# A gate block ahead of the latent attention's first scores, and one fewer behind its last

## The reference, cut to what matters

```python
z = h @ w_in + b_in            # 34 column chunks of 128, then four gates of 1024 columns
y_a = gmlp(u, v)               # spatial mixing within chunks of 128 tokens
y_b = short_conv(cb, cc, ch)
y_c = mla(q_lat, kv_lat, k_rope)   # latent attention: 8 heads, causal, query/key width 96, value width 64
y_d = nsa(nq, ...)                 # sparse attention: 16 head units
merged = sigmoid(ga)*y_a + sigmoid(gb)*y_b + sigmoid(gc)*y_c + sigmoid(gd)*y_d
mix = merged @ w_o
```

## Time and profile before

| | us |
|---|---|
| median of 3 runs | 2861.49 |
| lowest and highest | 2860.31, 2862.87 |
| the profiled execution's own time | 2865.89 |
| its span, first to last instruction | 2864.0 |
| TensorE busy in the span | 2712.1 (95%) |
| GpSimd busy | 2202.7 (77%) |
| ScalarE busy | 1492.4 (52%) |
| VectorE busy | 1359.3 (47%) |
| mean granted TensorE clock | 0.975 of full speed |

### The profile page before, as it was taken

The page is one execution under the profiler, slowest core; times in us unless marked ns, Lnnn a source line. Parts: engine busy times, 40 slices in busy tenths (PEclk is TensorE's granted clock), DMA queues, the critical chain, the costliest instruction groups (busy, mean ns, idle before and its releaser), DMA issues.

```text
span 2864.0 us, 60059 instructions
## 1 busy us (share of the span) xinstructions
PE 2712.1 (95%) x21781; PEld 2618.4 (91%) x21788; DVE 1359.3 (47%) x2507; ACT 1492.4 (52%) x2261; POOL 2202.7 (77%) x1681
## 2 busy tenths in 40 slices
PE   8999999999999999999999989998999899898997
PEld 8999988889999989998889989998999899788997
DVE  2125435646556554435556554246533533735334
ACT  4444445555555545455455554457544644555445
POOL 7875766757988967666758978978899699667994
PEclk9999999999999999999999999999999999999998
DMA  6554434434554544434434544544555455444552
GB/s 239 185 169 145 147 119 138 149 125 148 187 179 155 184 147 166 135 131 134 162 118 155 184 154 155 183 150 159 166 185 182 140 191 183 133 134 149 187 183 80
DMA packets 123000, 452.12 MB, mean 158 GB/s; under 512 B 13650, under 2 KB 13650, under 8 KB 122196
## 3 DMA queue, kind: packets, MB, share of 16 engines
q1 hardware_dynamic: 121104, 441.43, 46.3%
q10 hardware_dynamic: 1732, 8.39, 0.8%
HBM read 448.72 MB, written 1.05 MB: 157 GB/s over the span
## 4 chain that ended last, share of the span: by engine, by line
POOL 60%; issue 31%; PE 7%; POOLq 1%; DVE 0%; ACT 0%; DVEq 0%; ACTq 0%
POOL wl L373 31%; POOL wl L374 29%; PE R L412 2%; PE R L408 2%; PE R L411 2%; PE Y L408 1%; PE Y L412 1%; PE Y L411 1%; POOLq L379 0%; PE R L571 0%; POOLq L377 0%; DVE BL L1917 0%; DVE X L2042 0%; PE R L435 0%; ACT wh L1142 0%
## 5 line engine op out<-in xcount | busy, mean ns | idle before, releaser
L373 POOL TENSOR_TENSOR wl<-raw,wh 128x512 fp32r<-128x512 f32 x836 | 1111.8, 1330 | 636.8 <-ACT wh L1142 630.4
L408 PE MATMUL R<-XHB,wh 128*128 128x256 f32 (+1 forms) x4168 | 1191.5, 286 | 16.2 <-DVE XLB L2296 6.2
L412 PE MATMUL R<-XHB,wl 128*128 128x256 f32 (+1 forms) x4168 | 1182.3, 284 | 0.0
L411 PE MATMUL R<-XLB,wh 128*128 128x256 f32 (+1 forms) x4168 | 1178.5, 283 | 0.0
L374 POOL TENSOR_TENSOR wl<-raw,wh 128x512 fp32r<-128x512 f32 x836 | 1142.6, 1367 | 0.0
L1142 ACT ACTIVATE wh<-raw 128x1024 fp32r<-128x1024 f32 x836 | 877.1, 1058 | 300.2 <-PE R L408 219.9
L408 PEld LDWEIGHTS R<-XHB,wh 128*128 128x128 f32 x4168 | 792.6, 190 | 23.9 <-POOL wl L374 10.5
L411 PEld LDWEIGHTS R<-XLB,wh 128*128 128x128 f32 x4168 | 795.8, 191 | 1.8 <-issue 1.0
L412 PEld LDWEIGHTS R<-XHB,wl 128*128 128x128 f32 x4168 | 794.2, 191 | 0.0
L408 PE MATMUL Y<-BH,wh 128*128 128x256 f32 x1408 | 398.0, 283 | 1.3 <-DVE BL L1841 1.3
L412 PE MATMUL Y<-BH,wl 128*128 128x256 f32 x1408 | 396.4, 282 | 0.0
(11 more groups left out here) (409 smaller groups left out, 3204.6 us busy)
## 6 DMA issues: line engine op xcount, KB each, us to landing
raw<-in_stream SPq DMA_DIRECT2D x836, 512.0 KB, 3.3
G<-in_wcmp ACTq DMA_DIRECT2D x2, 2048.0 KB, 7.7
G<-in_mem ACTq DMA_DIRECT2D x2, 1024.0 KB, 5.9
TB<-in_table SPq DMA_DIRECT2D x1, 1312.0 KB, 12.8
X<-in_x SPq DMA_DIRECT2D x2, 512.0 KB, 5.9
out_dram<-X ACTq DMA_DIRECT2D x4, 256.0 KB, 2.2
WS<-in_mix_w ACTq DMA_DIRECT2D x2, 256.0 KB
G<-in_p ACTq DMA_DIRECT2D x2, 256.0 KB, 3.3
```

Source lines behind the costliest of these rows:

```text
L373: pool.tensor_tensor(wl[:, s, 0:512], raw[:, r, 0:512], wh[:, s, 0:512].bitcast(F32), ALU.subtract)
L408: i = pe.matmul(o, wh[w], hi, start=start, stop=False, skip_group_check=True)
L411: pe.matmul(o, wh[w], lo, start=False, stop=False, skip_group_check=True)
L412: i = pe.matmul(o, wl[w], hi, start=False, stop=stop, skip_group_check=True)
```

## The change

On TensorE one gate block is issued in front of the waits that precede the first scores, and the last head's filler has one block in place of two. The number of blocks and their order in the stream stay as they are, and so do the lists of all other engines.

```diff
+                dense(XH, XL)
                 pe.wait_ge(q_up, l + 1)
                 pe.wait_ge(kv_up, l + 1)
                 for b in range(4):
                     pe.wait_ge(aside_taken[b], ((l + 1) * len(ASIDE) - b + 3) // 4)
-                attention_pairs([mla_unit(h) for h in range(8)], lambda u: (dense(XH, XL), dense(XH, XL)))
+                attention_pairs([mla_unit(h) for h in range(8)], lambda u: [dense(XH, XL) for _ in range(2 if u < 7 else 1)])
```

## The result

The change took 2872.33 us (median of 7 runs, 2870.62 to 2877.22), the kernel before 2864.38 in the runs it is compared with (2860.31 to 2870.28). The ratio is 1.0033, with a 95% interval of 1.0023 to 1.0043, so +6.6 to +12.3 us. Forecast were +5.8 and 2867.3 in a range up to 2870.5. The time came out 5.0 above the forecast: 2.9 because before, in these runs, has a median of 2864.38 and not the 2861.49 that the forecast started from, and 2.1 because the medians lie 7.95 apart and not 5.8. Its profiled execution took 2872.33, span 2870.4; that of before 2865.89 and 2864.0.

A forecast was written before the change was run, and what follows sets the result against it. TensorE's own work was taken to set the pace inside the attention. Stalls less gains, +4.1 over both layers, plus one clock fall of 1.7 gave +5.8 on a median of 2861.5: 2867.3 us, range 2860.5 to 2870.5.

The forecast's parts named there:

- The gain of the moved block, 4.6 and 4.3: Before the second pair's transposes: us gained in first and second layer if nothing stalls, 8.9 together.
- The added wait at the third block, caused by ScalarE's list: In every pair TensorE waits for GpSimd's half of a block ScalarE rounds only after the exponentials; eight waits, about 2.5 or 1.2.
- The stall of 2.53 in the first pair: First layer, third block: ready at 379.78, wanted at 377.41, plus 0.16 for pick-up and a longer first matmul.
- 1.9 and 1.2 in the later pairs: Third-block stalls: 1.9 us in the first layer's second pair, 1.2 in each other later pair of both layers.
- One clock fall, 1.7, with bounds 0 and 3.4: Behind the first pairs' stalls TensorE's clock falls in one of two layers, adding 1.7 us.
- the rival with a fall in both layers: The stalls plus a clock fall in each layer: +7.5, 2869.0 us; chance 0.22.
- The sum of the stages, +5.8: Both attention stages: stalls less gains, +4.1, and one clock fall, 1.7, make the execution 5.8 us longer.
- The stage has no slack, and what the attention loses is passed on in full: Behind the attention TensorE sets the pace, so the attention's whole loss, +5.8 us, reaches the total.
- the difference is put on the median: 2867.3: The +5.8 was added to the median of the runs shown, 2861.5, not to the profiled execution.
- The bound of 5.7 us for faster, same, slower: What a measurement of the total can tell from no change, about 0.2%; the +5.8 lay on it.

The follow-up runs named there:

- a_5: The change unaltered, its fifth profiled execution: 2867.80 us, stages 67.53 and 68.94.
- first3: The change with the block in front taken from the first pair (three blocks there), not the last: 2864.06 against 2864.04, ratio 1.0005.
- layer0: The kernel before with the change in the first layer alone: 2865.25 against 2864.04, ratio 1.0005.
- layer1: The kernel before with the change in the second layer alone: 2867.40 against 2861.74, ratio 1.0025.
- the filled kernel: The change with ten matmuls of zeros on TensorE in front of the first pair's third block: 2870.13 against 2861.74, ratio 1.0030.
- Pad: The kernel before with twelve matmuls of zeros behind the latent attention in each layer: 2870.18 against 2861.74, ratio 1.0031.
- pad16: The kernel before with sixteen matmuls of zeros behind the first layer's latent attention alone: 2861.81 against 2863.00, ratio 1.0001.
- b_3: The kernel before, unchanged, its third profiled execution: 2861.29 us, stages 64.62 and 66.07.
- b_5: The kernel before, unchanged, its fifth profiled execution: 2855.34 us, stages 64.64 and 65.91.

## Why the prediction was wrong, step by step

- *The gain of the moved block, 4.6 and 4.3.* Right: without stalls the stages are 8.8 shorter, for 8.9.
- *The added wait at the third block, caused by ScalarE's list.* Right in cause and place: eight waits for L374, none when ScalarE's list moves along, one per layer when only the first pair leads.
- *The stall of 2.53 in the first pair.* Right: 2.24 idle and 0.16 for the pick-up and the longer first matmul, 2.40. The next transposes were put 0.80 later than before. Counted from the eviction of chunk 33 they came 0.85 later in a_5, where the clock stayed up, and 2.4 later in the first trace, where it fell.
- *1.9 and 1.2 in the later pairs.* The 1.9 was mis-sized: in before g7's second half ends 9.32 behind its own pair's scores (394.49 - 385.17), in the change 8.60 (394.44 + 1.27 - 387.11), as g11's does in before (408.43 - 399.81 = 8.62). From scores to scores a pair takes 402.84 - 387.11 = 15.73 in the change and 14.64 before, so each costs 1.1.
- *One clock fall, 1.7, with bounds 0 and 3.4.* Mis-sized: there were two, as in the rival with a fall in both layers, which had a chance of 0.22. The clock fell behind 13 of the 14 unfilled first-pair waits in the traces of the change, its four repeats, first3, layer0 and layer1. Each costs 1.5, by the filled kernel.
- *The sum of the stages, +5.8.* It was measured as +5.8 in the first pair of traces and as +6.2 over five of each. That it fits is luck: a second fall that was not in the sum, and later pairs that cost less than the sum had for them, cancelled each other.
- *"The stage has no slack, and what the attention loses is passed on in full", and "the difference is put on the median: 2867.3".* This is the step that failed, in two terms. The first is the clock in all the other stages, which the sum has at nothing, from one trace. It was not the same: the mean granted clock was 0.9780 before and 0.9756 in the change, which goes with 3.6 us; the 5.8 of the stages did arrive, as 6.9 (5.8 to 8.1) at the same clock. Pad shows the same without any stall: 5.0 in the stages, 8.4 in the total. The second is the median of three runs, 2861.49, taken with their 2.6 us as the kernel's spread. The later runs of before go from 2855 to 2870, and the median in the comparison was 2864.38. On that one the same +5.8 gives 2870.2, and the same range would have ended at 2873.4, above the measured 2872.33.
- *The bound of 5.7 us for faster, same, slower.* The forecast lay on it and the chances were split nearly evenly between same and slower; it came out slower.

What stays open is why the mean clock of the change is lower. The largest surplus found in a single stretch, the compression's, is not tied to the change, and a bare delay moved the mean clock both down (pad) and up (pad16).

## What to carry to other kernels

When one engine's work is moved forward by a unit, look at the lists of the engines that prepare its inputs. A lead of one block uses up one block of reserve for as long as it lasts; here moving the preparing instruction along turned a loss of 0.33% into a gain of 0.13%. And before a forecast of a few us is written, ask how much of the single trace is the state of the clock in that execution, and compare kernels at the same mean clock as well as by their medians: here 0.001 of it goes with 1.5 us.

## What the runs showed that I had not expected

The clock's falls are not a property of the kernel alone: behind the same gap of 2.75 us in front of the first scores, it stood at 0.50 in three traces of before and at 1.00 in two, b_3 and b_5. In the second layer, behind 2.53, it fell in all five. Behind the wait of 2.24 it was up once, in the first layer of a_5. The two stretches lie behind that wait, one after the other:

```profile
376.50:380.00 3.50, 3.50 (x32) 3.50 (x31) 0.00 (x0) 1.53 (x2) 3.46 (x4) 1.00 0.58 171
380.10:383.50 3.40, 3.40 (x29) 3.27 (x29) 0.00 (x0) 0.49 (x1) 3.40 (x3) 1.00 0.73 239
```

The compression's small matmuls have the clock at 0.50 without any gap: in the stretches above from 1117.90 (before, first trace) and from 1115.20 (b_3) TensorE is busy for all of the 3.10 and the 6.40 us.
